# Feed-forward order of VectorE and ScalarE, later key transposes and sample scores, and matmuls on constants during the token load

## The chip, the cores and the metric

The kernel runs on one core of a Trainium2 chip. Its engines are TensorE (PE, matmuls and transposes), VectorE (DVE, elementwise), ScalarE (ACT, activations and copies), GpSimd (POOL, here mostly a DMA queue) and SyncE (SP, the other DMA queue). The metric is the device time of one execution in microseconds (us), median of several runs. The engines run side by side, each through its own list in order, and hold each other up with semaphores.

## The reference

Two layers of an encoder trunk run for 512 new tokens (prompt) and 64 tokens of a later chunk (sample), 576 tokens in all, with width 1024. Everything is float32. Per layer:

```
def project(x, g_mix, w_in, q_norm, k_norm):
    z = rms_norm(x, g_mix) @ w_in                       # 1024 -> 3584
    qa, ka, va, qr, kr, vr, gr = jnp.split(z, cuts, axis=-1)
    qa = rms_norm(qa.reshape(B, L, HEADS_A, HEAD_DIM_A), q_norm)
    ka = rms_norm(ka.reshape(B, L, HEADS_A, HEAD_DIM_A), k_norm)
...
def merge_and_ffn(x, o_a, o_r, g_r, ret_norm, w_out, g_ffn, w_gate, w_up, w_down):
...
    x = x + jnp.concatenate([o_a, o_r], axis=-1) @ w_out
    h = rms_norm(x, g_ffn)
    return x + (jax.nn.silu(h @ w_gate) * (h @ w_up)) @ w_down     # 1024 -> 2816 -> 1024
```

Mixer A is softmax attention over 8 heads of 64 with a bias by distance; the sample's queries also see 512 cached keys. Mixer R is a retention over 4 heads of 128. The keys, the values and the retention states are outputs too.

## The kernel before

**Number format.** Activations and weights are held in a hi part (rounded to fp32r by an ACT copy, lines 593, 841, 814 to 829) and a lo part (the rest, by a DVE subtraction, lines 983, 1399, 1362 to 1371). A product is three passes: hi x hi, hi x lo, lo x hi. So each weight tile goes DMA, ACT hi, DVE lo, PE; the PE may start a tile only behind DVE's lo (`lo_done`, `f_lo_done`).

**Token load.** `x` comes in four pairs of column tiles. PE transposes tile k (`x_tiles(k)`, line 1709), DVE and ACT copy it out of PSUM (lines 1039, 635), ACT and DVE make its hi and lo (lines 598, 996), and unit 0 of W_in takes its weight pass k (line 1639) between the transposes of later tiles. Before the tokens are there PE multiplies zeros: 8 matmuls of 128 x 256 on `row_f` (line 1692). `in_lo(0, 0)` is DVE's lo of unit 0's weights.

**Attention.** The projections of mixer R run as "half units" (line 1771: 24 matmuls over half of the tokens), spread between the steps of attention to keep PE busy. Line 1685 transposes to tokens: group 1 is K, four head pairs of 128 columns for five token tiles, which ACT copies to `vr` (line 616). Then comes a loop over k of 20 items (4 head pairs p x 5 token tiles t, `STEPS_A` = 22 steps): `scores(k)` (L1825; for t = 4, the sample, L1832 to 1834 with the cached keys), a half unit where k is in `AT_A` (all k but those with k % 5 = 3), `probs(k - 1)` (transposes, L1847), `values(k - 2)` (L1867). DVE adds the bias and finds the least (`add_bias`, L1181), ACT takes exponentials (L723), DVE scales (L1194). `scores(k)` waits for the biases of item k - 1, because both use the same PSUM banks.

**Feed-forward.** W_gate and W_up are multiplied by a seven-product (Strassen-like) scheme over halves of the width and of the tokens. A pair n (of 11 in a group, 2 groups a layer) is one 128-column tile of gate and of up. Its seven products have the names A11, A12, A22 (weights as they are) and S1 to S4 (sums of weights, made by DVE, `weight_sum`, L1393). Each is 12 matmuls (L2044), in the order of `STEPS`; A22 of pair n comes behind A11 of pair n + 1. ACT copies the first product out (`product_1`, L871, `p1`) and the first corner (`corner_11`, L877); DVE makes `made_15` and `made_16` (L1457, L1464: product plus `p1`), the corners 12, 22 and 21 (L1471, L1478, L1483), `scale_gate` (L1488), `gate_up` (L1496) and the lo of the result (`act_low`, L1501); ACT takes silu (L881). S3's product waits for `made_16`, since it goes on in the same bank. `follow(n, name)` makes the next pair's hi (ACT) or lo (DVE) of a factor. ACT's order within a step is `product_1(n)`, silu of pair n - 1, then hi of A11, A22, S2, S1, `corner_11`, and on.

Before the first pair of group 0 the seven activation operands are made: `operand(c)` scales x[c] by the gain (L1345 for the upper four), ACT rounds (`operand_hi`, L817; `sum_hi`, L829), DVE takes the rest (`operand_lo`, L1365; `sum_lo`, L1371). Products wait for a count of `b_lo`. In the same stretch the row factors of the norm are found: squares, `rms_sums` and `rms_spread` on PE, root on ACT, inverse on DVE, and `rms_rows` on DVE, which copies them out of PSUM (L1014, L1015) for `scale_gate`.

What sets the order is the written program of each engine alone; no scheduler moves anything.

## Time and profile before

| | |
|---|---|
| median of 3 runs | 1494.76 us (1494.13 to 1495.31) |
| the profiled execution's own time | 1495.21 us |
| its span, first to last instruction | 1493.2 us |
| PE busy | 1459.1 us (98%) |
| DVE busy | 1016.7 us (68%) |
| ACT busy | 615.6 us (41%) |
| mean granted PE clock | 0.995 of full |

PE's share counts its matmuls as they overlap; the rest are waits. The other engines' shares are means over stages: in the feed-forward DVE is nearly always at work, in the down projection it idles. The clock column of the views is 1.00 at 2.4 GHz and 0.50 at 1.2 GHz.

### The profile page before, as it was taken

Reading aid. Unit: us, or ns where it says so; the run is one execution under the profiler, and the core shown is the slowest. Engines: PE = TensorE matmul, PEld = TensorE weight load, DVE = VectorE, ACT = ScalarE, POOL = GpSimd, SP = SyncE. Lnnn points to the kernel's source line nnn. Section 1 sums busy time; section 2 is a strip of 40 time slices with the busy share of each in tenths; the row PEclk is TensorE's granted clock in tenths of the full one; section 3 lists DMA queues with packets and bytes.
Section 4 is the critical chain, followed back from the end, with each engine's and each line's share of the span. In section 5 each row is a group of like instructions: output and inputs, shape, how many; then the busy total and the mean of one; then the engine's idle time right before and its main releaser. Section 6 shows DMA issues by size and latency. Waiting matters only on the chain. (4 is left out here: it accounts for less than half of the span.)

```text
span 1493.2 us, 29385 instructions
## 1 busy us (share of the span) xinstructions
PE 1459.1 (98%) x11053; PEld 1402.9 (94%) x11053; DVE 1016.7 (68%) x1977; ACT 615.6 (41%) x1072; POOL 43.6 (3%) x83
## 2 busy tenths in 40 slices
PE   8999999999999999999999999999999999999998
PEld 7998888999999999999999988898989999999998
DVE  5347764779998349995542777457799973699832
ACT  4223444345555115553332244444365541355411
POOL 0101100000000000000010011000000000000000
PEclk9999999999999999999999999999999999999999
DMA  4523311232333323333242143112333422333322
GB/s 143 157 70 114 95 57 54 81 97 70 86 84 95 97 75 86 100 89 97 67 141 85 57 121 92 49 56 82 85 86 85 112 78 78 85 103 95 87 86 76
DMA packets 225824, 132.72 MB, mean 89 GB/s; under 512 B 4664, under 2 KB 220656, under 8 KB 225728
## 3 DMA queue, kind: packets, MB, share of 16 engines
q1 hardware_dynamic: 220624, 114.11, 27.0%
q0 software_dynamic: 5008, 17.29, 3.8%
q8 instruction: 62, 1.02, 0.3%
q14 instruction: 34, 0.28, 0.1%
q10 hardware_dynamic: 96, 0.02, 0.0%
HBM read 123.23 MB, written 8.18 MB: 88 GB/s over the span
## 5 line engine op out<-in xcount | busy, mean ns | idle before, releaser
L1639 PE MATMUL ps<-act,hi_down 128*128 128x288 f32 x1408 | 245.1, 296 | 0.0
L1639 PE MATMUL ps<-mix,hi_of 128*128 128x288 f32 x1280 | 225.9, 299 | 4.8 <-DVE lo_of L983 4.2
L1771 PE MATMUL ps<-mix,hi_of 128*128 128x288 f32 x1024 | 211.3, 300 | 0.0
L1639 PEld LDWEIGHTS ps<-act,hi_down 128*128 128x128 f32 x1408 | 207.2, 189 | 0.0
L1639 PEld LDWEIGHTS ps<-mix,hi_of 128*128 128x128 f32 x1280 | 188.9, 190 | 7.8 <-issue 2.9
L1771 PEld LDWEIGHTS ps<-mix,hi_of 128*128 128x128 f32 x1024 | 162.6, 188 | 10.0 <-issue 6.6
L2044 PE MATMUL ps<-sums_b,hi_S 128*128 128x288 f32 x704 | 144.5, 298 | 9.4 <-DVE p_f L1464 8.8
L841 ACT ACTIVATE hi_S<-sum_S 128x512 fp32r<-128x512 f32 x176 | 110.0, 632 | 104.5 <-PE ps L2044 79.9
L1771 PE MATMUL ps<-mix,lo_of 128*128 128x288 f32 x512 | 150.8, 295 | 0.0
L1639 PE MATMUL ps<-act,lo_down 128*128 128x288 f32 x704 | 150.7, 296 | 0.0
L2044 PE MATMUL ps<-sums_a,hi_S 128*128 128x288 f32 x704 | 143.4, 296 | 0.0
L2044 PE MATMUL ps<-sums_a,hi_A 128*128 128x288 f32 x704 | 142.8, 295 | 0.0
L1639 PE MATMUL ps<-mix,lo_of 128*128 128x288 f32 x640 | 137.4, 297 | 0.0
L1514 DVE TENSOR_TENSOR work<-ps,row_f 128x576 f32<-128x576 f32 x32 | 24.3, 758 | 157.9 <-PE ps L1639 157.9
L2044 PEld LDWEIGHTS ps<-sums_b,hi_S 128*128 128x128 f32 x704 | 113.7, 190 | 10.7 <-DVE lo_A L1399 9.6
L1399 DVE TENSOR_TENSOR lo_S<-sum_S,hi_S 128x512 fp32r<-128x512 f32 x176 | 119.9, 686 | 0.1
L593 ACT ACTIVATE hi_down<-raw_down 128x1408 fp32r<-128x1408 f32 x32 | 44.3, 1384 | 171.4 <-PE ps L1639 161.5
L2044 PEld LDWEIGHTS ps<-sums_a,hi_S 128*128 128x128 f32 x704 | 113.8, 190 | 0.0
L1639 PEld LDWEIGHTS ps<-act,lo_down 128*128 128x128 f32 x704 | 113.4, 189 | 0.0
L2044 PEld LDWEIGHTS ps<-sums_a,hi_A 128*128 128x128 f32 x704 | 112.6, 188 | 0.5 <-issue 0.3
L983 DVE TENSOR_TENSOR lo_of<-raw_of,hi_of 128x1024 fp32r<-128x1024 f32 x72 | 87.9, 1221 | 33.4 <-ACT hi_of L593 33.2
L593 ACT ACTIVATE hi_of<-raw_of 128x1024 fp32r<-128x1024 f32 x72 | 75.8, 1053 | 74.6 <-PE ps L1639 55.1
(236 smaller groups left out, 2693.7 us busy)
## 6 DMA issues: line engine op xcount, KB each, us to landing
raw_of<-in_w_in SPq DMA_DIRECT2D x56, 512.0 KB, 3.7
raw_down<-in_w_down SPq DMA_DIRECT2D x32, 704.0 KB, 4.6
pair_raw<-in_w_gate SPq DMA_DIRECT2D x42, 512.0 KB, 4.0
pair_raw<-in_w_up SPq DMA_DIRECT2D x42, 512.0 KB, 5.2
raw_of<-in_w_out SPq DMA_DIRECT2D x16, 512.0 KB, 4.2
strip_even<-bias_lines POOLq DMA_DIRECT2D x8, 320.0 KB, 5.2
strip_odd<-bias_lines POOLq DMA_DIRECT2D x8, 320.0 KB, 5.5
stage<-in_x_prompt SPq DMA_DIRECT2D x4, 512.0 KB, 5.9
```

The lines of the kernel that those rows point to most:

```text
L593: nc.scalar.activation(dst[slot][:], src[slot][:], ACT.Copy).then_inc(hi_done, 1)
L841: nc.scalar.activation(f_hi[name].rearrange("p k n -> p (k n)"), src, ACT.Copy).then_inc(f_hi_done, 1)
L983: nc.vector.tensor_tensor(dst[slot][:], src[slot][:], high[slot][:].bitcast(F32), ALU.subtract).then_inc(lo_done, 1)
L1399: nc.vector.tensor_tensor(f_lo[name].rearrange("p k n -> p (k n)"), src, f_hi[name].rearrange("p k n -> p (k n)").bitcast(F32), ALU.subtra ...
L1514: nc.vector.tensor_tensor(halves(work[:, 1, :]), dense(s), halves(row_f[:]), ALU.mult).then_inc(down_scaled, 1)
L1639: last = nc.tensor.matmul(ps[:, bank + half, 0:HALF], weights(w, slot, nk)[:, k, :], src[:, k, part, HALF * half:HALF * half + HALF], star ...
L1771: last = nc.tensor.matmul(ps[:, half_bank(i), 0:HALF], weights(w, n % 2, KD)[:, k, :], mix[:, k, part, HALF * half:HALF * half + HALF], st ...
L2044: last = nc.tensor.matmul(ps[:, bank, 0:HALF], (f_hi, f_lo)[w][name][:, k, :], tile[:, at, k, part, :], start=start and k + i == 0, stop=k ...
```

## The change

- Token load: `keep_warm(4)` follows the transposes of tiles 1 and 2, on the zeros of `row_f`, into PSUM bank 3 (the first eight go there too). `in_lo(0, 0)` moves ahead of the wait for tile 2 and its copy.
- Attention: K's transposes to tokens stand behind the first scores and a half unit; ACT's copies of them stand behind the first exponentials. Scores of the sample (k % 5 = 4) stand behind their half unit.
- Feed-forward, group 0: x[7] times gain is made by ACT (`operand_last`), `sum_lo(1)` stands ahead of `made_16`, and `rms_rows` of this norm is ACT's. Both groups: `corner_12` of the first pair stands between sums S1 and S2, and ACT's `corner_11` of the first pair behind the hi of A11 and A22. In every pair: DVE's lo of A11 stands between the sums S1 and S2.

```diff
@@ ACT, attention
-                for t in range(TT):
-                    tok_copy(l, 1, vr, t)
...
                     if k < NA:
                         exponentials(k)
+                    if k == 0:
+                        for t in range(TT):
+                            tok_copy(l, 1, vr, t)
                     if 1 <= k <= NA:
                         probs_out(k - 1)
@@ ACT, feed-forward
+                def operand_last():
+
+                    c = KD - 1
+                    eng.wait_ge(evacuated, x_count(l, 1) + c + 1)
+                    eng.wait_ge(b_lo, (KD + 4) * l + c - 1)
+                    nc.scalar.activation(h_f[:, h_row(c), :], x[:, c, :], ACT.Copy, scale=gain[:, KD + c:KD + c + 1]).then_inc(h_set, 1)
+
...
+                def rms_rows(l):
+
+                    eng.wait_ge(rms_bcast, 2 * l + 2)
+                    nc.scalar.activation(row_f[:, 0:SEQ], ps[:, 7, :], ACT.Copy)
+                    nc.scalar.activation(row_f[:, SEQ:TOK], ps[:, 6, P:P + DEC], ACT.Copy).then_inc(rms_row, 1)
...
                     if c == U_OUT - 1:
+                        operand_last()
                         eng.wait_ge(w_used, U_LAYER * l + FIRST_DOWN + RING)
                         sum_hi(0, slice(0, KH - 1), 2 * KH - 2)
                     operand_hi(c)
...
-                    corner_11(first)
...
                     for name in STEPS:
                         follow(first, name)
+                        if name == "A22":
+                            corner_11(first)
+                            if g == 0:
+                                rms_rows(l)
@@ DVE
             for k in range(KD):
+                if k == 2:
+                    in_lo(0, 0)
                 dve.wait_ge(x_ps, k + 1)
                 nc.vector.tensor_copy(x[:, k, 0:SEQ], ps[:, 4 + 2 * (k % 2), :]).then_inc(evacuated, 1)
                 if k:
-                    if k == 2:
-                        in_lo(0, 0)
                     norm_lo(0, 0, mix, k - 1)
...
-                    operand(c)
+                    if c < U_OUT - 1:
+                        operand(c)
...
                     first_pair_lo(g, FIRST_PAIRS[g][4:])
+                    if g == 0:
+                        sum_lo(1, slice(0, KH), 3)
                     made_16(first)
                     if g == 0:
-                        sum_lo(1, slice(0, KH), 3)
+                        sum_lo(2, slice(0, KH), 4)
                         rms_invert(l, 1)
-                        sum_lo(2, slice(0, KH), 4)
...
                     weight_sum(g, first.next(), "S1")
+                    corner_12(first)
                     weight_sum(g, first.next(), "S2")
-                    corner_12(first)
                     corner_22(first)
...
-                    if g == 0:
-                        rms_rows(l, 1)
                     follow(first, "S3")
                     follow(first, "S4")
+                    if g == 0:
+                        dve.wait_ge(rms_row, 2 * l + 2)
                     scale_gate(first)

                     def steps(n):
                         weight_sum(g, n.next(), "S1")
+                        follow(n, "A11")
                         weight_sum(g, n.next(), "S2")
-                        follow(n, "A11")
                         corner_21(n.prev())
@@ PE
-            for i in range(8):
-                nc.tensor.matmul(ps[:, 7, 0:2 * P], row_f[:, 0:P], row_f[:, 0:2 * P], start=True, stop=True)
+            def keep_warm(n):
+                for i in range(n):
+                    nc.tensor.matmul(ps[:, 3, 0:2 * P], row_f[:, 0:P], row_f[:, 0:2 * P], start=True, stop=True)
+
+            keep_warm(8)
...
             for k in range(3):
                 x_tiles(k)
+                if k:
+                    keep_warm(4)
...
-                pe.wait_ge(qk_normed, 8 * l + 8)
-                to_tokens(l, 1, qk[:, 4:8, :])
...
-                pe.wait_ge(tok_evac, 3 * TT * l + 2 * TT)
+                pe.wait_ge(qk_normed, 8 * l + 2)
                 for k in range(STEPS_A):
-                    if k < NA:
+                    late = k % TT == QT
+                    if k < NA and not late:
                         scores(k)
                     if k in AT_A:
                         half_unit(PRE + AT_A.index(k))
+                    if k < NA and late:
+                        scores(k)
+                    if k == 0:
+                        pe.wait_ge(qk_normed, 8 * l + 8)
+                        to_tokens(l, 1, qk[:, 4:8, :])
+                    if k == 1:
+                        pe.wait_ge(tok_evac, 3 * TT * l + 2 * TT)
```

On DVE, in the feed-forward, one step of the pairs, before. `sum_S` are the sums of weights (109 is S1's, 110 is S2's), `lo_A_103` the lo of A11, `lo_A_108` that of A22, `work<-ps,p_f` a corner, `work<-work,row_f` is `scale_gate`:

```order
L1488 TENSOR_TENSOR work<-work,row_f 128x576
L1393 TENSOR_TENSOR sum_S_109<-pair_raw_92 128x512
L1393 TENSOR_TENSOR sum_S_110<-sum_S_109,pair_raw_92 128x512
L1399 TENSOR_TENSOR lo_A_103<-pair_raw_92,hi_A_97 128x512
L1483 TENSOR_TENSOR work<-ps,p_f 128x288
L1399 TENSOR_TENSOR lo_A_108<-pair_raw_93,hi_A_107 128x512
```

The same place now, with the line numbers of the changed kernel:

```order
L1505 TENSOR_TENSOR work<-work,row_f 128x576
L1409 TENSOR_TENSOR sum_S_109<-pair_raw_92 128x512
L1415 TENSOR_TENSOR lo_A_103<-pair_raw_92,hi_A_97 128x512
L1409 TENSOR_TENSOR sum_S_110<-sum_S_109,pair_raw_92 128x512
L1500 TENSOR_TENSOR work<-ps,p_f 128x288
L1415 TENSOR_TENSOR lo_A_108<-pair_raw_93,hi_A_107 128x512
```

The lo of A11 has moved ahead of the sum S2; what follows keeps its order.

On PE, around the sample's scores of the first head pair, before (`kc_t,qbd` are the cached keys and the sample's queries, `mix` a half unit):

```order
L1825 MATMUL ps<-qk,q_rev 128x512 x2
L1847 MATMUL ps<-cst,sc 128x128 x6
L1867 MATMUL ps<-pt,va 64x128 x4
L1832 MATMUL ps<-kc_t,qbd 128x288
L1833 MATMUL ps<-kc_t,qbd 128x224
L1834 MATMUL ps<-qk,qbd 128x64
L1771 MATMUL ps<-mix,hi_of_82 128x288 x2
L1771 MATMUL ps<-mix,lo_of_84 128x288
```

Now the end of that half unit and what follows it:

```order
L1794 MATMUL ps<-mix,hi_of_82 128x288 x2
L1794 MATMUL ps<-mix,lo_of_84 128x288
L1851 MATMUL ps<-kc_t,qbd 128x288
L1852 MATMUL ps<-kc_t,qbd 128x224
L1853 MATMUL ps<-qk,qbd 128x64
L1866 MATMUL ps<-cst,sc 128x128 x8
L1886 MATMUL ps<-pt,va 64x128 x6
L1844 MATMUL ps<-qk,q_rev 128x128 x2
```

The 24 matmuls of the half unit now lie ahead of the sample's scores, and only the transposes and values of earlier items lie between these and the next item's scores.

On PE, in the token load, now (before, the two rows on `row_f` were not there; `cst,stage` are transposes of tokens, `hi_of` and `lo_of` unit 0):

```order
L1730 MATMUL ps<-cst,stage 128x128 x4
L1730 MATMUL ps<-cst,stage 128x64
L1711 MATMUL ps<-row_f 128x256 x4
L1730 MATMUL ps<-cst,stage 128x128 x4
L1730 MATMUL ps<-cst,stage 128x64
L1711 MATMUL ps<-row_f 128x256 x4
L1657 MATMUL ps<-mix,hi_of_82 128x288 x4
L1657 MATMUL ps<-mix,lo_of_84 128x288 x2
```

Four matmuls on zeros stand behind tile 1 and four behind tile 2, ahead of unit 0's first pass.

## Rows read from the trace of the kernel before

**Rows 1.** The page, part 1: busy us (share of the span), instructions.
```profile
PE 1459.1 (98%) x11053; PEld 1402.9 (94%) x11053; DVE 1016.7 (68%) x1977; ACT 615.6 (41%) x1072; POOL 43.6 (3%) x83
```

**Rows 2.** PE's waits, whole span: line, releaser, us in total, times, longest.
```profile
PE ps L2044 <- DVE p_f L1464: 8.8, 4, 2.6
...
PE ps L1832 <- DVE least L1181: 2.3, 8, 0.3
...
PE ps L1825 <- ACT vr L616: 1.9, 2, 1.0
PE ps L1685 <- DVE qk L1136: 1.9, 2, 0.9
```

**Rows 3.** Table of stretches: us, busy (instructions) of each engine, clock, DMA.
```profile
13.90:20.30 6.40, 6.37 (x24) 5.45 (x25) 2.61 (x4) 1.23 (x3) 0.00 (x0) 0.50 0.74 231
...
382.20:385.50 3.30, 3.30 (x16) 3.30 (x15) 3.30 (x7) 2.05 (x4) 0.00 (x0) 0.50 0.99 263
```

**Rows 4.** Timeline, token load: start, us, engine, line, operation; idle before in brackets.
```profile
1.73 6.15 PE L1692 MATMUL ps<-row_f 128*128 128x256 f32 x16 [1.73 <-DVE row_f L1021]
...
12.66 1.22 DVE L983 TENSOR_TENSOR lo_of<-raw_of,hi_of 128x1024 fp32r<-128x1024 f32 x1
...
13.93 1.33 PE L1639 MATMUL ps<-mix,hi_of 128*128 128x288 f32 x4 [1.92 <-DVE lo_of L983]
...
23.24 0.79 PE L1639 MATMUL ps<-mix,hi_of 128*128 128x288 f32 x4
...
24.87 0.79 PE L1639 MATMUL ps<-mix,hi_of 128*128 128x288 f32 x4
```

**Rows 5.** Timeline, the sample's first scores, PE and DVE.
```profile
149.34 0.72 PE L1832 MATMUL ps<-kc_t,qbd 128*128 128x288 f32 x2 [0.29 <-DVE least L1181]
...
155.47 0.49 PE L1825 MATMUL ps<-qk,q_rev 64*128 64x128 f32 x4
...
153.92 0.76 DVE L1181 CUSTOM_DVE_ANT_0 sc<-ps,strip_even 64x576 f32<-64x576 f32 x1
```

**Rows 6.** Timeline, first products of group 0, layer 0; L598 from the token load.
```profile
358.74 0.52 DVE L1345 TENSOR_SCALAR h_f<-x,gain 128x576 f32<-128x576 f32 x1
...
360.14 0.75 DVE L1365 TENSOR_TENSOR sums_a<-h_f,sums_a 128x576 fp32r<-128x576 f32 x1
...
365.70 0.46 DVE L1464 TENSOR_TENSOR p_f<-ps,p_f 128x288 f32<-128x288 f32 x1 [1.01 <-PE ps L2044]
...
375.16 0.69 DVE L1014 COPY row_f<-ps 128x512 f32<-128x512 f32 x1
...
357.94 0.93 ACT L829 ACTIVATE sums_b<-t_f 128x864 fp32r<-128x864 f32 x1 [2.99 <-PE ps L1639]
...
9.79 0.78 ACT L598 ACTIVATE mix<-x,gain 128x576 fp32r<-128x576 f32 x1 [0.66 <-DVE x L1039]
...
381.50 0.50 PE L2044 MATMUL ps<-sums_b,hi_S 128*128 128x288 f32 x2 [2.64 <-DVE p_f L1464]
```

**Rows 7.** Timeline, first products of group 1, DVE.
```profile
565.75 1.29 DVE L1399 TENSOR_TENSOR lo_A<-pair_raw,hi_A 128x512 fp32r<-128x512 f32 x2 [2.09 <-ACT hi_A L841]
```

**Rows 8.** Timeline, one round of the loop over pairs, DVE, then ACT.
```profile
454.75 0.76 DVE L1488 TENSOR_TENSOR work<-work,row_f 128x576 f32<-128x576 f32 x1
...
456.25 0.69 DVE L1393 TENSOR_TENSOR sum_S<-sum_S,pair_raw 128x512 f32<-128x512 f32 x1
456.86 0.68 DVE L1399 TENSOR_TENSOR lo_A<-pair_raw,hi_A 128x512 fp32r<-128x512 f32 x1
...
462.04 0.69 DVE L1399 TENSOR_TENSOR lo_A<-pair_raw,hi_A 128x512 fp32r<-128x512 f32 x1 [0.33 <-ACT hi_A L841]
...
465.85 0.76 DVE L1488 TENSOR_TENSOR work<-work,row_f 128x576 f32<-128x576 f32 x1
...
455.53 0.69 ACT L881 ACTIVATE work<-work 128x576 f32<-128x576 f32 x1 [0.39 <-DVE work L1488]
456.13 1.14 ACT L841 ACTIVATE hi_A<-pair_raw 128x512 fp32r<-128x512 f32 x2
```

More of the change, by code:

```diff
@@ L1009, in rms_invert, with rms_rows @@
                 nc.vector.reciprocal(inv[0:DEC, QT:TT], root[0:DEC, QT:TT]).then_inc(rms_inv, 1)
-            def rms_rows(l, which):
-                dve.wait_ge(rms_bcast, 2 * l + which + 1)
+            def rms_rows(l):
+                dve.wait_ge(rms_bcast, 2 * l + 1)
                 nc.vector.tensor_copy(row_f[:, 0:SEQ], ps[:, 7, :])
                 nc.vector.tensor_copy(row_f[:, SEQ:TOK], ps[:, 6, P:P + DEC]).then_inc(rms_row, 1)
-                dve.wait_ge(rms_row, 2 * l + which + 1)
+                dve.wait_ge(rms_row, 2 * l + 1)
             dve.sem_inc(lo_done, RING)
@@ L1062, in _ @@
                 unit_lo(3)
-                rms_rows(l, 0)
+                rms_rows(l)
                 for n in range(2):
```

## Prediction

> **What bounds the kernel now.** I read the page's busy shares first. TensorE (PE) multiplies for 98% of the span [rows 1], so only what stands in its way can be saved: its waits, and stretches at the lower of its two clock levels. The table of waits names them [rows 2]: 8.8 us for DVE's `p_f` sums in the feed-forward, 2.3 for the score biases, 1.9 each for the copies of K's token tiles and for the last normalised K. The clock's table has PE at half speed (1.2 instead of 2.4 GHz) behind idle stretches: 13.9 to 20.3 us and 382.2 to 385.5 us [rows 3], with the same again in layer 1. I then read each place in time order.
>
> **Token load.** One step of it (a weight pass of unit 0 and the transposes of a later tile) takes 24.87 - 23.24 = 1.63 us at full clock [rows 4]. From pass 0 (13.93) to pass 5 (24.87) it is 10.94, most of it at half clock; five full-clock steps are 8.15. So holding the clock gives 2.8. The work that should hold it are 2 x 4 matmuls of zeros. Eight of them took 6.15 at the start, most of it at half clock [rows 4], so four at full clock are an estimated 1.7 (3.1 at most). The first four start behind tile 1 at about 9.6 and end at 11.3, where tile 2 started at 11.15 before; tile 2 needs some 0.8 and the next four end at 13.9. DVE's lo part of unit 0 is moved ahead of tile 2's copy and now ends near 12.9 instead of 12.66 + 1.22 = 13.9 [rows 4]; the zeros use that up, so pass 0 starts at 13.9 as before, but at full clock. DVE's copy and lo of a tile fit in 1.63: PE had no gap at 23.24. All that follows hangs on the tiles and shifts along. Gain 2.8; bounds 0 (the clock falls all the same) and 3.8 (PE also gets the microsecond of the lo part).
>
> **K's token transposes** (both layers). They stood between the last half unit and the first scores; PE idled 0.94 for the last K before them and 0.96 for ACT's copies behind them (the 1.9 and 1.9 of [rows 2] are two layers each), and each restart costs some 0.1 more. Now the first scores and a whole half unit run first, and a half unit covers the copies. What is late next? ACT takes the first exponentials ahead of the five copies, but PE needs the copies' result only behind the second half unit. The weights of the unit after it hang on scores, evacuation and lo, which all move together. Nothing comes in its place: 2.15 a layer, 4.3 in all; bounds 3.8 and 4.6.
>
> **The sample's scores** (four a layer) now stand behind their half unit. PE's 0.29 wait for the biases [rows 5], 2.3 in all by [rows 2], goes with a restart of 0.15: 0.44 each. But DVE's two bias passes of 0.77 each ended at 154.68 (the second from 153.92 [rows 5]); now they start with the scores' end, at about 153.5, and end at 155.04. PE wants the next scores at 155.47 - 0.44 = 155.03 and must wait till 155.2, with a restart of 0.1. That leaves 0.2 for three of the four, 0.44 for the last (no scores follow it): 1.0 a layer, 2.1 in all; bounds 0 and 3.5.
>
> **First products, group 0.** S3 of pair 1 waits 2.64 us for `p16` [rows 6]. DVE runs without a pause from 367 to that point, so its queue is what counts, from the last unit of W_out on.
> - x[7] times gain goes to ACT. On DVE it was 0.52 [rows 6]; on ACT the same form is 0.78 [rows 6]. It stands ahead of ACT's `sum_hi(0)`, which could run at 357.94 while DVE still added to x. Now ACT waits for x till 358.7, scales (0.7 to the next start), rounds the sums (0.93) and ends at 360.3; DVE idles, and its lo of the last operand, on which A12 hangs, starts at 361.3 instead of 360.14 [rows 6]: PE waits 1.15 at A12, and DVE's queue is 1.15 later.
> - The lo of the second sums fills DVE's idle 1.01 ahead of `p16` of pair 0 [rows 6]: -1.0.
> - The copies of the row sums go to ACT: 0.69 + 0.22, 0.85 of DVE's queue [rows 6]: -0.85. PE's short gaps at pair 0 shrink, which only lengthens the wait behind them.
> - The new order inside a step costs DVE 0.5 (next part), and the waits around the swapped corner 0.2.
>
> Sum 1.15 - 1.0 - 0.85 + 0.5 + 0.2 = 0: S3 of pair 1 starts when it did, PE idles 2.7 there again and the clock falls again, as at 382.2.
>
> **First products, group 1.** DVE idles 2.09 for ACT's hi of A11 [rows 7], since ACT stands at `corner_11`, which waits for A12's product. With the corner behind the two hi's this idle goes, but 1.0 and 0.6 of it come back as waits for S4's and S3's products in the two corners; with the 0.15 that the spread sums save, the queue gains 0.86. The step's new order takes 0.5 back: S3 of pair 1 waits some 0.3 less than the 1.74 that make up the rest of [rows 2]'s first row.
>
> **The loop over pairs** (the part that speaks against the change). One round takes 465.85 - 454.75 = 11.10 [rows 8], which is PE's seven products. DVE waits inside it only for ACT's hi of A12 and for its own sum S1, and would need 10.70. The change puts the lo of A11 between sums S1 and S2. ACT makes the hi of A11 behind the silu, and the silu waits for `scale_gate` at the round's start: silu starts 0.78 in, hi of A11 1.38 in, which ends 2.00 in (0.62 of the 1.14 for two), and DVE can start 2.04 in [rows 8]. Before, the sums S1 (from 0.67 in) and S2 (from 1.50 in, 456.25) filled that time, and the lo of A11 started 2.11 in (456.86). Now DVE idles from 1.36 to 2.04, and S2's 0.6 comes after. The rest of the round, from the lo of A11 to the next `scale_gate`, is 465.85 - 456.86 = 8.99, less the 0.41 that A12's hi held it up (0.33 of it shown as idle at 462.04), plus 0.6 for S2: 9.19. So DVE's round is 2.04 + 9.19 = 11.23: 0.5 longer than the 10.70 of before and 0.12 longer than PE's 11.11. Where PE has just waited for `p16` there is no slack, and each of the 8 rounds up to pair 9 costs PE 0.12: 1.0 a group. In group 0 the half-clock stretch (PE 1.7 late) pays for it, if it stays. So group 0 comes to 0, group 1 to +1.0 - 0.3 = +0.7; both layers +1.4. Bounds: -6 (the new order costs nothing, which gives 1.5 in each of four groups) and +5.
>
> On the swap itself rows and page differ. S2's sum starts 0.84 behind S1's (0.67 and 1.50 in), where the next follows S2 in 0.61 [rows 8]: waiting for the own engine's semaphore costs 0.24. The Trainium skill (VectorE: DVE Perf Modes, section The DRAIN you can't avoid) says that a semaphore between two chained operations costs nothing extra. By the row the swap takes 0.24 out of DVE's round, by the page 0; under both the idle for ACT's hi swallows it and the round stays 11.23, so the trace decides nothing against the sum here.
>
> **Sum.** -2.8 - 4.3 - 2.1 + 1.4 = -7.8. The profiled execution took 1495.21 (span 1493.2 and 2.0 around it): 1487.4. The median of the three runs is 0.45 lower: 1487.0.
>
> **Rivals.**
> 1. The new order in the loop does no harm (ACT's hi comes in time, or DVE's slack covers it). For it: DVE idles 0.33 a round, and its lo parts are ready some 6 us before PE needs them. Against it: `p16` has no such lead behind a wait. Then 1.4 turns into up to -4: 1482.
> 2. The clock falls at the token load although PE is busy: no 2.8, 1490. Against it: the same zeros raised it at the start.
> 3. The half-clock stretches of group 0 vanish, because the wait falls at another moment: 1.7 less each, but the 1.0 of the loop comes back: -0.7 each, 1485.5. The wait of 1.74 in group 1 was followed by no fall.
> 4. Slower. DVE's and ACT's round is longer than my 11.23, say because ACT's hi of A22, S2 and S1 queue behind the same silu and each makes DVE wait. There are 32 such rounds; the other terms bring 9.2, less the 1.5 of group 0's half clock. Slower by over 3.0 needs 12.2 / 32 = 0.38 over PE's 11.11, a round of 11.49; at 11.55 the time is 1499.
> 5. The change does not do what it says: the new waits of the scores and of A12 eat attention's gain, and the clock falls at the start: 1492.5, no measurable change.
>
> **How the numbers follow.** A measurement of this kernel tells 0.2% (3.0 us) from no change. The forecast, with rival 3's small step inside it, has 0.6; rival 1 has 0.17, rival 2 has 0.08, rival 5 has 0.08, rival 4 has 0.05, and 0.02 are left. Faster: 0.6 + 0.17 + 0.08 + 0.01 = 0.86; the same 0.08; slower 0.06. The range from 1481.5 (rival 1) to 1491 (rival 2 with attention at its lower bound) leaves rivals 4 and 5 out.
>
> **What would show it.** Full clock through the token load, and pass 0 at 13.9; PE without a gap of 0.9 around the K transposes, small ones of 0.2 at the scores behind the sample's; a PE gap of about 1.2 at A12 of group 0's pair 0 for DVE's `sums_a`; a wait of 2.6 to 2.8 at S3 of pair 1 in group 0 and 1.4 in group 1; in the pairs behind, DVE idle 0.7 for `hi_A` between two sums, and rounds of 11.23 where PE waits 0.1 for `p_f` each time. If the rounds read 11.11, the loop term was wrong; if the gap at A12 is not there, ACT's place for the scaling was.

## The result and the profile after

| | kernel before | changed kernel |
|---|---|---|
| median | 1494.76 us | 1486.73 us (5 runs, 1486.50 to 1487.29) |
| the profiled execution's own time | 1495.21 | 1487.29 |
| its span | 1493.2 | 1485.5 |

The ratio is 0.9946, with a 95% interval of 0.9932 to 0.9961: 8.0 us faster. The forecast was 1487.0. Line numbers below are those of the changed kernel: its matmuls of the seven products are L2071 (L2044 before), `made_16` is L1481, `weight_sum` L1409, the lo parts L1415, `scale_gate` L1505, ACT's hi parts L853, silu L894.

The page, part 1. PE's share is still 98%, 1460.0 us against 1459.1 [rows 1], with 16 records more (the profile has two for each of the 2 x 4 matmuls on zeros):

```profile
PE 1460.0 (98%) x11069; PEld 1404.8 (95%) x11069; DVE 1010.1 (68%) x1971; ACT 614.0 (41%) x1078; POOL 43.4 (3%) x83
```

PE's waits over the whole span (line, releaser, us in total, times, longest):

```profile
PE ps L2071 <- DVE p_f L1481: 8.1, 4, 2.5
PE ps L2071 <- DVE sums_a L1381: 2.3, 2, 1.2
```

Against [rows 2], the 2.3 for `least` and, at K's transposes, the 1.9 for `vr` and the 1.9 for `qk` are gone. `p_f` has gone from 8.8 to 8.1 only, and `sums_a` is new: 1.15 in each layer, where the forecast put it.

The table of stretches (us, busy of each engine, then clock and DMA) at the places of [rows 3]: token load, then behind S3 of pair 1 in group 0 of layer 0 and of layer 1.

```profile
13.90:20.30 6.40, 6.40 (x45) 5.62 (x44) 4.01 (x7) 2.76 (x7) 0.00 (x0) 1.00 0.70 222
375.90:379.30 3.40, 3.40 (x25) 3.40 (x26) 3.40 (x7) 2.14 (x4) 0.00 (x0) 1.00 0.76 217
1102.20:1109.00 6.80, 6.19 (x26) 6.22 (x27) 6.19 (x13) 2.45 (x5) 0.00 (x0) 0.50 0.57 157
```

Full clock at the first two, where the kernel before had 0.50; at the third the half-clock stretch is there and twice as long as before.

Timeline of the token load, PE and then DVE. The second zeros end at 14.2 and pass 0 starts at 14.26, at full clock; the lo part ended at 12.78, so the zeros decide. Tile 2 starts at 11.82, behind a wait for its DMA (11.15 in the kernel before).

```profile
11.82 0.86 PE L1730 MATMUL ps<-cst,stage 128*128 128x128 f32 x5 [0.34 <-DMA stage<-in_x_sample]
12.61 2.00 PE L1711 MATMUL ps<-row_f 128*128 128x256 f32 x8
14.26 0.88 PE L1657 MATMUL ps<-mix,hi_of 128*128 128x288 f32 x4
...
11.55 1.23 DVE L999 TENSOR_TENSOR lo_of<-raw_of,hi_of 128x1024 fp32r<-128x1024 f32 x1 [0.23 <-ACT hi_of L593]
```

The last short wait of the load ends at 28.81 before (first line) and at 26.43 now. The experiments below use this wait's end as the end of the load.

```profile
28.81 0.79 PE L1639 MATMUL ps<-mix,hi_of 128*128 128x288 f32 x4 [0.30 <-DVE lo_of L983]
```

```profile
26.43 0.80 PE L1657 MATMUL ps<-mix,hi_of 128*128 128x288 f32 x4 [0.30 <-DVE lo_of L999]
```

Timeline of attention, PE: K's 20 transposes start with no idle ahead of them, and the scores behind the sample's wait 0.12 (150.73 less the end at 149.73 + 0.88), where before it was 0.29 ahead of the sample's own [rows 5].

```profile
129.84 2.35 PE L1703 MATMUL ps<-cst,qk 128*128 128x128 f32 x20
...
149.73 0.88 PE L1886 MATMUL ps<-pt,va 128*64 128x128 f32 x12
150.73 0.49 PE L1844 MATMUL ps<-qk,q_rev 64*128 64x128 f32 x4
```

Behind attention PE waits for `q_rev`, in both kernels; the wait begins at 239.81 before and at 234.31 now, by times that are not rounded. It ends where the first line starts (before) and where the second does (now):

```profile
240.71 0.52 PE L1685 MATMUL ps<-cst,vt 128*128 128x128 f32 x3 [0.91 <-ACT q_rev L697]
```

```profile
235.21 0.96 PE L1703 MATMUL ps<-cst,vt 128*128 128x128 f32 x7 [0.90 <-ACT q_rev L693]
```

Timeline of the first products of group 0: ACT, DVE, PE. The scaling of x[7] and the rounding of the sums behind it end at 354.81; PE gets A12 at 356.72. At 375.86 stands S3 of pair 1.

```profile
353.22 0.78 ACT L814 ACTIVATE h_f<-x,gain 128x576 f32<-128x576 f32 x1 [3.78 <-DVE x L1343]
353.90 0.91 ACT L841 ACTIVATE sums_b<-t_f 128x864 fp32r<-128x864 f32 x1
...
354.84 1.06 DVE L1387 TENSOR_TENSOR sums_b<-t_f,sums_b 128x864 fp32r<-128x864 f32 x1 [1.66 <-ACT sums_b L841]
355.82 0.75 DVE L1381 TENSOR_TENSOR sums_a<-h_f,sums_a 128x576 fp32r<-128x576 f32 x1
...
356.72 0.50 PE L2071 MATMUL ps<-sums_a,hi_A 128*128 128x288 f32 x2 [1.15 <-DVE sums_a L1381]
...
375.86 0.50 PE L2071 MATMUL ps<-sums_b,hi_S 128*128 128x288 f32 x2 [2.54 <-DVE p_f L1481]
```

Timeline of group 1 of layer 0, DVE's two corners and a round, ACT's silu and hi, and S3 of pair 1 on PE:

```profile
560.10 0.46 DVE L1488 TENSOR_TENSOR work<-ps,p_f 128x288 f32<-128x288 f32 x1 [0.92 <-PE ps L2071]
...
561.68 0.46 DVE L1495 TENSOR_TENSOR work<-ps,p_f 128x288 f32<-128x288 f32 x1 [0.53 <-PE ps L2071]
...
566.27 0.75 DVE L1505 TENSOR_TENSOR work<-work,row_f 128x576 f32<-128x576 f32 x1
566.94 0.68 DVE L1409 TENSOR_TENSOR sum_S<-pair_raw 128x512 f32<-128x512 f32 x1
568.29 0.69 DVE L1415 TENSOR_TENSOR lo_A<-pair_raw,hi_A 128x512 fp32r<-128x512 f32 x1 [0.67 <-ACT hi_A L853]
568.90 0.68 DVE L1409 TENSOR_TENSOR sum_S<-sum_S,pair_raw 128x512 f32<-128x512 f32 x1
...
577.48 0.75 DVE L1505 TENSOR_TENSOR work<-work,row_f 128x576 f32<-128x576 f32 x1
...
567.05 0.69 ACT L894 ACTIVATE work<-work 128x576 f32<-128x576 f32 x1 [1.55 <-DVE work L1505]
567.64 1.14 ACT L853 ACTIVATE hi_A<-pair_raw 128x512 fp32r<-128x512 f32 x2
...
571.07 0.50 PE L2071 MATMUL ps<-sums_b,hi_S 128*128 128x288 f32 x2 [1.49 <-DVE p_f L1481]
```

DVE's idle of 2.09 [rows 7] has become 0.92 and 0.53. In the round, DVE waits 0.67 for ACT's hi of A11 between the sums S1 and S2. The round is 577.48 - 566.27 = 11.21, and all rounds of the four groups up to pair 10 read 11.20 to 11.22 (the last of a group is shorter), but for the first two of layer 1's group 0, which hold the half clock (12.27 and 11.48).

### The profile page after: what moved, and what is told of

It reads as the page before. It is cut to its first block and busy times, and to the rows that moved or that the text cites. A ratio compares the mean times of both kernels' runs of the same rounds, so it can differ in the third digit from the quotient of the medians.

```text
span 1485.5 us, 29415 instructions
## 1 busy us (share of the span) xinstructions
PE 1460.0 (98%) x11069; PEld 1404.8 (95%) x11069; DVE 1010.1 (68%) x1971; ACT 614.0 (41%) x1078; POOL 43.4 (3%) x83
## 3 DMA queue, kind: packets, MB, share of 16 engines
q8 instruction: 62, 1.02, 0.3%
## 5 line engine op out<-in xcount | busy, mean ns | idle before, releaser
L2071 PE MATMUL ps<-sums_b,hi_S 128*128 128x288 f32 x704 | 145.2, 299 | 8.1 <-DVE p_f L1481 8.1
L853 ACT ACTIVATE hi_S<-sum_S 128x512 fp32r<-128x512 f32 x176 | 107.2, 629 | 92.8 <-DVE sum_S L1409 60.6
L2071 PE MATMUL ps<-sums_a,hi_A 128*128 128x288 f32 x704 | 142.8, 296 | 2.3 <-DVE sums_a L1381 2.3
L2071 PE MATMUL ps<-sums_a,hi_S 128*128 128x288 f32 x704 | 144.6, 298 | 0.0
L2071 PEld LDWEIGHTS ps<-sums_b,hi_S 128*128 128x128 f32 x704 | 113.1, 190 | 9.1 <-DVE lo_A L1415 8.9
L1415 DVE TENSOR_TENSOR lo_S<-sum_S,hi_S 128x512 fp32r<-128x512 f32 x176 | 118.9, 680 | 0.9 <-ACT hi_S L853 0.9
L2071 PEld LDWEIGHTS ps<-sums_a,hi_A 128*128 128x128 f32 x704 | 112.9, 189 | 2.8 <-issue 2.7
L2071 PEld LDWEIGHTS ps<-sums_a,hi_S 128*128 128x128 f32 x704 | 113.2, 190 | 0.2
```

Source lines behind the costliest of these rows:

```text
L853: nc.scalar.activation(f_hi[name].rearrange("p k n -> p (k n)"), src, ACT.Copy).then_inc(f_hi_done, 1)
L1415: nc.vector.tensor_tensor(f_lo[name].rearrange("p k n -> p (k n)"), src, f_hi[name].rearrange("p k n -> p (k n)").bitcast(F32), ALU.subtra ...
L2071: last = nc.tensor.matmul(ps[:, bank, 0:HALF], (f_hi, f_lo)[w][name][:, k, :], tile[:, at, k, part, :], start=start and k + i == 0, stop=k ...
```

## The experiments

**The loop's order taken back.**

```diff
@@ DVE, steps(n)
                         weight_sum(g, n.next(), "S1")
-                        follow(n, "A11")
                         weight_sum(g, n.next(), "S2")
+                        follow(n, "A11")
```

> The changed kernel with one part of it taken back: in the feed-forward's loop DVE makes the weight sum S2 ahead of the lo of A11 again, as before the change. Theory of the prediction (DVE idles 0.7 us a round for ACT's hi of A11, its round is 11.21 instead of 10.7, and PE, which waits for `p16` in every round up to pair 9, pays for it): DVE's rounds read 10.7 in the first four or five pairs of a group and 11.11 behind them, the waits of 0.1 at S3 go, and each of the four groups ends 1.5 us earlier: 5.8 us less, 1480.9. Rival (rounds are PE's own 11.11 plus something that the order does not touch): rounds stay 11.2, 1486.7 +- 0.5. Second rival (the lo of A11 in its old place makes the wait at S3 of pair 1 longer): no gain either, and the wait of 2.54 there reads 2.9 or more.

Measured: 1481.79 us (1479.52 to 1482.82), 4.9 below the changed kernel. The kernel before was measured again beside each batch of four kernels: 1495.18 beside this one and the next three; 1494.83 beside the fastest kernel, the one without zeros, and the two that change attention alone; 1494.56 beside the other four. PE's waits for `p_f` in the table of waits:

```profile
PE ps L2071 <- DVE p_f L1481: 6.0, 4, 2.1
```

DVE's rounds in group 1 of layer 0, timeline:

```profile
566.13 0.75 DVE L1505 TENSOR_TENSOR work<-work,row_f 128x576 f32<-128x576 f32 x1
566.79 0.69 DVE L1409 TENSOR_TENSOR sum_S<-pair_raw 128x512 f32<-128x512 f32 x1
567.63 0.69 DVE L1409 TENSOR_TENSOR sum_S<-sum_S,pair_raw 128x512 f32<-128x512 f32 x1
568.24 0.68 DVE L1415 TENSOR_TENSOR lo_A<-pair_raw,hi_A 128x512 fp32r<-128x512 f32 x1
...
576.82 0.75 DVE L1505 TENSOR_TENSOR work<-work,row_f 128x576 f32<-128x576 f32 x1
```

The idle is gone and the round is 10.69 (the first four rounds of this group read 10.69, then comes one of 11.05, then PE's 11.11). Both rivals fall: the order alone made the rounds 11.21, and the waits at S3 of pair 1 are shorter, not longer (2.07 and 1.99 in the two groups 0, 0.97 in both groups 1).

**x[7] times gain back on DVE.**

```diff
@@ ACT, the last unit of W_out
                     if c == U_OUT - 1:
-                        operand_last()
@@ DVE
-                    if c < U_OUT - 1:
-                        operand(c)
+                    operand(c)
```

> The changed kernel with one part of it taken back: x[7] times gain is DVE's again (ACT goes straight to its rounding of the sums). Theory: the scaling in ACT's queue made DVE's queue 1.2 us later, so PE's gap of 1.15 at A12 of group 0's pair 0 goes, and S3 of pair 1 waits 2.5 still or a little less (its `p16` is 1.2 us earlier, but so is PE): 1.2 us less in each layer, 1484.3; and 3.4 less on top (1481) if the half-clock stretch of 6.8 us in layer 1 goes with it. Rival (the gap at A12 is only the wait at S3 moved forward, and DVE saves the 0.43 of the scaling): the gap goes, the wait at S3 of pair 1 grows from 2.54 to 3.7, the time stays 1486.7.

Measured: 1484.29 us (1483.97 to 1484.61), 2.4 less. The gap at A12 is gone and the wait at S3 of pair 1 stays (2.59 and 2.55), so DVE and PE both moved forward by 1.2. The rival, in which the wait grows to 3.7, is out. The half clock behind S3 of pair 1, layer 0 and layer 1:

```profile
374.70:378.10 3.40, 3.40 (x25) 3.40 (x26) 3.40 (x7) 2.14 (x4) 0.00 (x0) 1.00 0.76 218
1100.60:1103.90 3.30, 3.16 (x13) 3.19 (x14) 3.30 (x6) 1.50 (x3) 0.00 (x0) 0.50 0.67 196
```

**Both taken back.** The two diffs above in one kernel.

> The changed kernel with both parts taken back: the loop's order S1, S2, lo of A11, and x[7] times gain on DVE. Theory (the two costs lie one behind the other in DVE's queue and add): 5.8 + 2.4 = 8.2 us less than the changed kernel, 1478.5, or 1475 if no half-clock stretch is left in group 0. Rival (one slack covers both): 1481.

Measured: 1478.40 us (1477.60 to 1479.06), 8.3 below the changed kernel. The costs add: the two differences above make 7.4 together before rounding, 0.9 less than this. The 0.9 is not separated; this trace has no half-clock stretch behind the token load at all (mean granted clock 1.0), where that of the loop's order alone has one of 3.4 us in each group 0. Even so the time is 1478.4, not 1475.

**ACT's hi of A11 ahead of the silu,** DVE's order as changed.

```diff
@@ ACT, steps(n)
                         product_1(n)
-                        silu(n.prev())
                         follow(n, "A11")
+                        silu(n.prev())
```

> The changed kernel with ACT's order inside a round changed: the hi of A11 ahead of the silu; DVE's order stays the changed one (S1, lo of A11, S2). Theory (the new DVE order costs time only because the hi of A11 stands behind the silu, which hangs on `scale_gate` at the round's start): DVE's idle of 0.7 between S1 and the lo of A11 goes, its round is 10.5, and each group ends 1.7 us earlier (the own-semaphore wait of S2 on S1 is saved too): 6.8 less, 1479.9. Rival 1 (the silu, now 0.6 later, makes `gate_up` wait): rounds stay at 11.2 with DVE's idle at `gate_up`, 1486.7. Rival 2 (the order on DVE is harmful by itself): rounds 11.2, 1486.7, without an idle of 0.7.

Measured: 1479.80 us (1479.73 to 1480.48), 6.9 less. PE's waits for `p_f`, and then DVE's same round in the timeline:

```profile
PE ps L2071 <- DVE p_f L1481: 5.0, 4, 1.8
```

```profile
565.36 0.75 DVE L1505 TENSOR_TENSOR work<-work,row_f 128x576 f32<-128x576 f32 x1
566.02 0.69 DVE L1409 TENSOR_TENSOR sum_S<-pair_raw 128x512 f32<-128x512 f32 x1
566.63 0.69 DVE L1415 TENSOR_TENSOR lo_A<-pair_raw,hi_A 128x512 fp32r<-128x512 f32 x1
567.23 0.69 DVE L1409 TENSOR_TENSOR sum_S<-sum_S,pair_raw 128x512 f32<-128x512 f32 x1
...
575.81 0.75 DVE L1505 TENSOR_TENSOR work<-work,row_f 128x576 f32<-128x576 f32 x1
```

The lo of A11 starts 0.61 behind the sum S1 with no idle, and the round is 10.45: shorter than with the old order (10.69), since S2's sum no longer waits out the own engine's semaphore (0.60 to 0.61 between starts against 567.63 - 566.79 = 0.84 above). So DVE's new order is not harmful; its place behind ACT's silu was. `gate_up` does not wait for the later silu (rival 1).

**Both at once: hi of A11 ahead of the silu, and x[7] times gain on DVE.**

```diff
@@ ACT
-                        operand_last()
...
-                        silu(n.prev())
                         follow(n, "A11")
+                        silu(n.prev())
@@ DVE
-                    if c < U_OUT - 1:
-                        operand(c)
+                    operand(c)
```

> The changed kernel with two edits: ACT's hi of A11 ahead of the silu, and x[7] times gain back on DVE. Theory (the two costs are separate: one is DVE's place in the first products of group 0, 1.2 us a layer, the other its rounds, 1.7 a group): 2.4 less than with the first edit alone (1479.8), 1477.4, and no wait at S3 of pair 1 in group 1; rival (PE bound already, DVE's gain is swallowed by its slack): 1479.8. Against the kernel with both parts taken back (1478.4) it should be 1.0 faster.

Measured: 1476.53 us (1476.23 to 1480.91), beside 1494.83 of the kernel before on that chip: ratio 0.9883 (0.9866 to 0.9899). The gain over the hi alone is 3.3, not 2.4; the half-clock stretch that the hi kernel's trace had in layer 0 is absent here, and had taken 1.5 between the two S3 of that layer (195.11 there, 193.57 here), while the wait for `o_tok` in layer 1 is 0.2 longer here (1.10 against 0.90). The forecast of no wait at S3 of pair 1 in group 1 was wrong: it is 0.73, as with the hi alone. It is the fastest kernel of this study, 10.2 below the changed one.

Against both parts taken back it is 1.9 faster by the medians, but the intervals of the two ratios overlap (0.9873 to 0.9903 there), and in the traces 1.25 of the difference is the load alone: tile 2 starts at 12.43 there and at 11.23 here. These are the end of the load and PE's last wait, for `x`, with both parts taken back and then here:

```profile
27.00 0.79 PE L1655 MATMUL ps<-mix,hi_of 128*128 128x288 f32 x4 [0.30 <-DVE lo_of L998]
...
1472.24 0.76 PE L2142 MATMUL ps<-cst,x 128*128 128x128 f32 x5 [1.21 <-DVE x L1532]
```

```profile
25.75 0.79 PE L1655 MATMUL ps<-mix,hi_of 128*128 128x288 f32 x4 [0.30 <-DVE lo_of L998]
...
1469.92 0.76 PE L2142 MATMUL ps<-cst,x 128*128 128x128 f32 x5 [1.21 <-DVE x L1532]
```

That is 1445.24 and 1444.17, with full clock all the way in both: 1.07, the 1.0 that was expected.

**No zeros in the token load.**

```diff
@@ PE
                 x_tiles(k)
-                if k:
-                    keep_warm(4)
```

> The changed kernel without the 2 x 4 matmuls of zeros between the transposes of tiles 1 and 2; `in_lo(0, 0)` keeps its new place ahead of tile 2's copy. Theory (the zeros hold the clock; the move of the lo part alone brings PE's pass 0 forward by 1.0): pass 0 starts at 12.9 instead of 14.26, but the clock falls at about 13.5 for 6.8 us as in the kernel before, and everything behind is 1.0 earlier than before instead of 2.4: 1.4 slower than the changed kernel, 1488.1. Rival (the shorter idle alone keeps the clock up, the zeros only cost PE time): full clock from 7 us on, 1.3 faster than the changed kernel, 1485.4.

Measured: 1485.71 us (1485.10 to 1486.04): 1.0 faster than the changed kernel, not 1.4 slower. Timeline, PE, and then the row of the half clock in the table of stretches:

```profile
11.06 0.86 PE L1730 MATMUL ps<-cst,stage 128*128 128x128 f32 x5 [1.67 <-DMA stage<-in_x_sample]
12.67 1.08 PE L1657 MATMUL ps<-mix,hi_of 128*128 128x288 f32 x4 [0.75 <-DVE lo_of L999]
```

```profile
13.00:16.40 3.40, 3.40 (x15) 2.93 (x14) 1.92 (x4) 1.19 (x3) 0.00 (x0) 0.50 1.09 348
```

Both theories miss. The clock falls, but for 3.4 us and not for 6.8, and pass 0 starts 1.6 earlier than with the zeros. The last short wait of the load ends at 26.25, against 26.43 with the zeros and 28.81 before. The rest of the 2.1 between the two spans (1485.5 and 1483.4) is the stretch of layer 1, which this trace does not have.

The same comparison on the fastest kernel:

> The fastest kernel so far (hi of A11 ahead of the silu, x[7] times gain on DVE) without the 2 x 4 matmuls of zeros. Theory from the trace without zeros (the lo part's new place brings nearly all of the gain, the zeros shorten the way from tile 2's start to the last short gap of the load by 0.6 but make tile 2 start up to 0.4 later): within 0.5 of the kernel with them, 1476.5 +- 0.5. Rival 1 (the zeros cost more than they bring, as the medians 1485.7 without and 1486.7 with them suggest): 1475.5. Rival 2 (the half-clock stretch at 13 us costs its full 1.7): 1478.2.

Measured: 1477.77 us (1477.62 to 1478.45), 1.2 above 1476.53. Here the lo part ends later and pass 0 starts at 13.18, and the clock still falls to half at 14.0, for 3.4 us; the load's last wait ends at 26.77 against 25.75. The expected 1476.5 and its rivals 1475.5 and 1478.2 leave this between the first and the last: with the lo part moved, the zeros are worth between -0.2 and 1.0 at the end of the load. Counted from tile 2's start, which came 0.5 to 0.8 earlier without them, they are worth 0.6 and 1.5.

**The lo part of unit 0 back behind tile 2's copy,** the zeros as changed.

```diff
@@ DVE, token load
-                if k == 2:
-                    in_lo(0, 0)
                 dve.wait_ge(x_ps, k + 1)
...
                 if k:
+                    if k == 2:
+                        in_lo(0, 0)
                     norm_lo(0, 0, mix, k - 1)
```

> The changed kernel with the lo part of unit 0 back behind the copy of tile 2; the 2 x 4 matmuls of zeros stay. Theory (the zeros hold the clock, and pass 0 waits for the lo part as it did before, 2.8 behind tile 2's start instead of 2.4): full clock through the load, 0.3 slower than the changed kernel, 1487.0. Rival (the gain of the token load is the lo part's new place, and the clock falls in the wait that this opens): half clock at 13 to 20 us, 1.5 to 2.5 slower, 1488.7.

Measured: 1486.05 us (1484.88 to 1487.75), the same as the changed kernel within its runs. Timeline, PE, and the stretch behind it, at full clock through the load as the theory said:

```profile
10.96 0.86 PE L1730 MATMUL ps<-cst,stage 128*128 128x128 f32 x5
11.74 1.99 PE L1711 MATMUL ps<-row_f 128*128 128x256 f32 x8
13.73 0.79 PE L1657 MATMUL ps<-mix,hi_of 128*128 128x288 f32 x4
```

```profile
13.00:20.30 7.30, 7.30 (x49) 5.94 (x47) 5.66 (x8) 3.41 (x7) 0.00 (x0) 1.00 0.83 242
```

From tile 2's start to the end of the load's last wait it takes 14.83 (10.96 to 25.79). The same distance in the other traces:

| | zeros | no zeros |
|---|---|---|
| lo part ahead of tile 2's copy | 14.5 to 14.6 (eight traces) | 15.19, 16.06 |
| lo part behind it | 14.83 | 17.66 (before), 17.77, 18.10 |

Of the gain of 3.05 by both edits, the zeros alone bring 2.8 and the lo part alone 2.5 and 1.6, in its two traces; the two do not add. Tile 2's start itself ranges over the traces from 10.68 to 12.43: in ten of the fourteen PE waits there for the DMA, in the other four, all with zeros, it starts as soon as the zeros ahead of it are done. A median can't tell 0.3 here.

**K's transposes alone,** on the kernel before: the part of the diff on `to_tokens`, its waits and ACT's copies of `vr`; the diff here shows `to_tokens` only.

```diff
@@ PE
-                pe.wait_ge(qk_normed, 8 * l + 8)
-                to_tokens(l, 1, qk[:, 4:8, :])
...
                         half_unit(PRE + AT_A.index(k))
+                    if k == 0:
+                        pe.wait_ge(qk_normed, 8 * l + 8)
+                        to_tokens(l, 1, qk[:, 4:8, :])
```

> The kernel before with one part of the change alone: K's transposes to tokens behind the first scores and a half unit, ACT's copies of them behind the first exponentials. Theory: both gaps of 0.94 and 0.96 with their restarts go and nothing comes in their place: 2.15 in each layer, 4.3 less than before in all, ratio 0.9971. Rival (the first exponentials and copies in ACT's queue come late for the weights' hi part, or values for V's bank): half of it, 2.1, with a new gap of 0.5 to 1 behind the second half unit.

Measured: 1490.64 us (1487.37 to 1493.62), ratio 0.9960 (0.9946 to 0.9974), 4.2 below 1494.83. The runs scatter by 6 us. In this trace, the slowest of them, tile 2 came at 12.10 and the half clock lasted 10.2 us in the load and 6.8 in group 0 of layer 0. So attention is better read by itself: from the load's last wait to the wait for `q_rev` it took 239.81 - 28.81 = 211.00 before, and 239.03 - 30.20 = 208.83 here: 2.17 in layer 0, and 2.22 between the same places in layer 1. Nothing takes the place of the gaps.

**The sample's scores alone,** on the kernel before: `late`, and the scores behind the half unit.

```diff
@@ PE
-                    if k < NA:
+                    late = k % TT == QT
+                    if k < NA and not late:
                         scores(k)
                     if k in AT_A:
                         half_unit(PRE + AT_A.index(k))
+                    if k < NA and late:
+                        scores(k)
```

> The kernel before with one part of the change alone: the sample's scores behind their half unit. Theory: four gaps of 0.29 at the sample's scores and their restarts go in each layer, three gaps of 0.13 come at the scores behind them, since DVE's bias passes now start later: 1.0 a layer, 2.1 less in all, ratio 0.9986. Rival 1 (the wait only moves to the next scores): same time as before, gaps of 0.3 at the next scores. Rival 2 (no new gap): 3.5 less.

Measured: 1492.48 us (1491.26 to 1496.43), ratio 0.9985 (0.9976 to 0.9994). The same distance is 238.47 - 28.45 = 210.02: 0.98 in layer 0, with three gaps of 0.13 at the next scores, and 1.02 in layer 1. The changed kernel has 234.31 - 26.43 = 207.88, 3.12 less than before: the two parts add (2.17 + 0.98).

**Two parts of group 0 taken back.**

```diff
@@ ACT, first pair
-                            if g == 0:
-                                rms_rows(l)
@@ DVE
-                    if g == 0:
-                        sum_lo(1, slice(0, KH), 3)
                     made_16(first)
                     if g == 0:
-                        sum_lo(2, slice(0, KH), 4)
+                        sum_lo(1, slice(0, KH), 3)
                         rms_invert(l, 1)
+                        sum_lo(2, slice(0, KH), 4)
...
                     follow(first, "A12")
+                    if g == 0:
+                        rms_rows(l, 1)
...
-                    if g == 0:
-                        dve.wait_ge(rms_row, 2 * l + 2)
```

> The changed kernel with two parts of group 0 taken back: the lo of the second sums behind `made_16` of the first pair again, and the copies of the row sums (`rms_rows`) on DVE again. Theory (each lengthens DVE's queue up to `p16` of pair 1, by 1.0 and 0.85): the wait at S3 of pair 1 in group 0 grows by what the two add less what PE loses at the first pair, and S3 of pair 1 starts 1.8 later in each layer: 3.7 slower in all, 1490.4. Rival (with the row copies in ACT's queue something else of ACT was late, so that taking them back costs less): 1.0 later in each layer, 1488.7. Group 1 should not change.

Measured: 1491.48 us (1489.76 to 1491.90), 4.8 slower. PE's waits for `p_f` in the table of waits:

```profile
PE ps L2068 <- DVE p_f L1479: 10.0, 4, 3.5
```

From A12 to S3 of pair 1 it takes 21.11 in both layers, against 375.86 - 356.72 = 19.14: 1.97, a little over the 1.85. How it divides between the two parts was not tested. Group 1 keeps its wait of 1.49. Twice 1.97 is 3.9; where the other 0.8 of the medians comes from stays open, since the trace is that of the fastest of the eleven runs (1489.76).

**ACT's `corner_11` of the first pair back in its old place.**

```diff
@@ ACT
+                    corner_11(first)
                     for name in STEPS:
                         follow(first, name)
                         if name == "A22":
-                            corner_11(first)
```

> The changed kernel with ACT's `corner_11` of the first pair ahead of the hi of A11 and A22 again. Theory: in group 1 DVE idles 2.1 again for the hi of A11 and gets back the waits at the corners, so S3 of pair 1 waits 1.0 longer (2.5 instead of 1.49); in group 0 it starts 0.25 later: 2.5 slower in all, 1489.2. Rival (DVE's idle is only moved): 1486.7, the wait at S3 of pair 1 in group 1 stays 1.5.

Measured: 1489.14 us (1488.27 to 1490.35), 2.4 slower. The same row of the table of waits:

```profile
PE ps L2071 <- DVE p_f L1481: 10.3, 4, 2.7
```

The waits at S3 of pair 1 in the groups 1 are 2.48 instead of 1.49, and A12 to S3 in group 0 takes 19.41 instead of 19.14, as reckoned.

## Why the prediction was right, point by point

The sizes below are differences of the two profiled executions at the same places, but for the two terms of attention, which come from the kernels that change one of them alone. Terms of a group count four times, those of group 1 or of a layer twice. They add up to the 7.7 between the spans, to 0.1.

| term | forecast | measured |
|---|---|---|
| token load | -2.8 | -2.4 (28.81 to 26.43) |
| K's transposes | -4.3 | -4.3 (2 x 2.17, alone) |
| the sample's scores | -2.1 | -2.0 (2 x 0.98, alone) |
| group 0 up to S3 of pair 1 | 0 | -0.13 a layer |
| group 1, wait at S3 of pair 1 | -0.3 | -0.25 (1.74 to 1.49) |
| rounds of a group | +1.0 | +0.76 |
| half clock in group 0 | -1.0 in each layer (it stays and pays for the rounds) | -1.5 in layer 0, +0.4 in layer 1 |
| wait for `o_tok`, layer 1 | - | -0.3 |

**Token load.** The mechanism held (full clock from 6.5 us on), the size was off. The step that failed is "the next four end at 13.9": tile 2 came 0.67 later than before, 0.34 of it behind the zeros' end for its DMA, so pass 0 started at 14.26. From pass 0 to the end of the load the gain was 2.7 (14.88 to 12.17), as forecast; counted from tile 2 it was 3.05. The forecast also gave all of it to the zeros; the runs with one edit each show that moving the lo part alone brings 1.6 to 2.5 of it, since pass 0 then starts earlier and the half clock lasts 3.4 us instead of 6.8.

**Attention.** Both terms stand to 0.1, including the small new waits behind the sample's scores. The edits tested alone add up to what both bring.

**First products.** The gap of 1.15 at A12 stood as worked out, and taking x[7] back gave 2.4 for two layers. The terms of -1.0 and -0.85 were 1.97 together; the corner's swap was worth 1.0 in group 1. They cancelled as forecast, and S3 of pair 1 started 0.13 earlier.

**The loop.** The round was 11.21 (forecast 11.23). Without the half clock and with all else equal, from S3 of pair 1 in group 0 to the same in group 1 takes 195.24 with the new order (x[7] on DVE, layer 0) and 193.88 with the old (both parts taken back): 1.36 a group, 0.52 at S3 itself and 0.84 in the rounds, for the forecast's 0.5 and 1.0. This is the part that rival 1 took for harmless. It costs 5.4 us in four groups: 4.9 and 5.9 in the two pairs of medians.

**Half clock.** "The clock falls again, as at 382.2" failed. Behind 2.54 us of idle it did not fall in layer 0; behind the same 2.54 in layer 1 it fell for 6.8 us. Rival 3 came true in one layer and its reverse in the other. With the old order a stretch of 3.4 costs 1.4 to 1.5 between those S3 (196.18 in the kernel before, 194.71 in the kernel with the sample's scores alone, whose layer 0 has none). With the new order it costs 0.5 to 0.7 (195.75 against 195.24 with x[7] on DVE, 195.86 against 195.19 with two parts of group 0 taken back), and the 6.8 of the changed kernel 1.9 (197.09 against 195.21): rounds set by DVE leave PE 0.1 each in which to catch up. That a stretch of 3.4 would pay for the rounds did hold where one stood: 195.75 is 0.2 less than the 196.16 of before without the 0.25 of group 1's wait. But the changed kernel's trace had none in one layer and a longer one in the other, so the terms of group 0 came to -0.9 in layer 0 and +1.0 in layer 1, for a forecast of 0 and 0. That the total is within 0.3 is in part luck: these two cancel, and the 0.4 missing at the load is made up by the two groups 1, each 0.2 shorter than forecast, and by the wait for `o_tok`, which was not in the forecast.

## What to carry to other kernels

Before a step is moved forward on one engine, follow what it waits for back to the round's start on the other: here the lo part was moved ahead of an ACT result that stood behind the silu, and moving that result with it turned a loss of 5.4 us against the old order into a gain of 1.1 over it by the distance inside the traces (1.9 by the medians, 1476.5 and 1478.4). A profile that is 98% busy still hides such costs, since the bound engine's waits are a tenth of a microsecond each; compare the period of the engine that feeds it with its own. Where the order of two parts is in doubt, try them alone, and read each by distances inside the trace, since the time as a whole carries the landing of one DMA and the clock's stretches.

## What the runs showed of the hardware

**Equal waits, unequal clock.** PE's idle at S3 of pair 1 in group 0 is the same in both layers to 0.1, and lies between 1.75 and 3.53 over the 14 traces. In 13 of these 28 places a stretch at 0.50 follows (10 of 3.4 us, 3 of 6.8), in 15 none. It followed idle times of 1.84 (the hi ahead of the silu, layer 0) and was absent behind 3.53 (two parts taken back, layer 1). So the length of this wait alone does not decide. Nor does length explain group 1: behind its 28 waits at S3 of pair 1 (0.73 to 2.5) the clock never fell, 2.48 included. The Trainium skill (TensorE: Matmul & The Clock Gate, section What's actually happening) says that the monitor behind the clock runs freely and is not reset when a kernel starts; by that rule the moment of a wait counts beside its length, and these traces agree, without proving it.

**The own engine's semaphore costs a quarter of a microsecond.** S2's sum starts 0.84 behind S1's when it waits for it, and any of them 0.60 to 0.61 behind the one ahead of it when another lies between. The Trainium skill (VectorE: DVE Perf Modes, section The DRAIN you can't avoid) says that the semaphore between chained operations costs nothing extra; by the rows here, 128 x 512 in float32, it costs 0.23, and the round with the other operation between the two sums was 0.24 shorter, 10.45 against 10.69. The measurement decides.
